# Attention pairs with two groups of keys: the gate products in two pieces of 12 instead of three of 8

## What is computed

```
y_c = chunk_band_attention(...)   # C: softmax(q k^T / 8 + bias) v, over at most 640 keys
y_a = dsa_mixer(...)              # A: softmax over the 256 best-scored of up to 1024 keys, times v
gates = sigmoid(h @ w_gate)       # 1024 x 4096, computed beside the attention
mixed = sum(gates * up, axis=branch)
```

## Time and profile before

| | before |
|---|---|
| median of 3 runs | 1749.71 us |
| the profiled execution | 1752.26 us |
| its span, first to last instruction | 1750.5 us |
| mean granted TensorE clock | 0.986 |
| TensorE matmul busy | 1683.8 us, 96% |
| VectorE busy | 1439.9 us, 82% |
| ScalarE busy | 938.0 us, 54% |
| GpSimd busy | 117.4 us, 7% |

### The profile page before, as it was taken

One profiled execution on the slowest core, in us unless ns is written; L12 is line 12 of the kernel. 1 busy time (PEld: TensorE's weight loads), 2 busy tenths in 40 slices (PEclk: granted clock), 3 DMA queues, 4 the chain that ended last, 5 costly groups with the idle time before them and its releaser, 6 DMA issues. The chain is left out here.

```text
span 1750.5 us, 24119 instructions
## 1 busy us (share of the span) xinstructions
PE 1683.8 (96%) x8776; PEld 1271.7 (73%) x8776; DVE 1439.9 (82%) x2045; ACT 938.0 (54%) x1218; POOL 117.4 (7%) x137
## 2 busy tenths in 40 slices
PE   7999999999999999999999999999999999999990
PEld 7768888877677777777778888867777777777760
DVE  6687958989799988678828986789888989898997
ACT  6533122133444545555566532277777787877762
POOL 1100000000000000000000000032211010000003
PEclk9999999999999999999999999999999999999995
DMA  5202132122354422412316841399999999999967
GB/s 210 72 1 85 54 108 92 61 85 73 108 189 131 140 69 67 145 55 67 127 37 238 304 172 66 137 381 393 403 397 404 393 404 392 404 394 402 405 270 288
DMA packets 77041, 359.82 MB, mean 206 GB/s; under 512 B 9021, under 2 KB 11613, under 8 KB 50589
## 3 DMA queue, kind: packets, MB, share of 16 engines
q1 hardware_dynamic: 67372, 325.14, 49.8%
q0 software_dynamic: 5888, 20.97, 3.5%
q10 hardware_dynamic: 3696, 12.59, 1.8%
HBM read 301.63 MB, written 55.99 MB: 204 GB/s over the span
## 5 line engine op out<-in xcount | busy, mean ns | idle before, releaser
L2805 DVE TENSOR_TENSOR wa_lo<-wa,w_hi 128x2048 fp32r<-128x2048 f32 x124 | 281.6, 2284 | 15.8 <-ACT w_hi L2689 14.9
L2689 ACT ACTIVATE w_hi<-wa 128x2048 fp32r<-128x2048 f32 x124 | 237.5, 1917 | 83.3 <-DMA wa<-expert_up 73.8
L1608 PE MATMUL psum<-h_hi,w_hi 128*128 128x512 f32 x510 | 210.0, 412 | 3.2 <-ACT gate_out L1270 2.7
L1608 PE MATMUL psum<-h_hi,w_lo 128*128 128x512 f32 x510 | 204.2, 400 | 0.0
L1608 PE MATMUL psum<-h_lo,w_hi 128*128 128x512 f32 x510 | 202.3, 397 | 0.0
L176 DVE MAX8 top<-sel 128x8 f32<-128x384 f32 (+5 forms) x192 | 171.3, 892 | 4.6
L174 DVE MATCH_REPLACE8 sel<-top,sel 128x384 f32<-128x384 f32 (+5 forms) x192 | 168.2, 876 | 0.0
L2813 DVE TENSOR_TENSOR wb_lo<-wd,w_hi 128x2048 fp32r<-128x2048 f32 x62 | 139.4, 2289 | 30.9 <-ACT w_hi L2699 30.9
L2585 PE MATMUL psum<-w_hi,xT_hi 128*96 128x512 f32 x508 | 162.2, 400 | 0.1
L2585 PE MATMUL psum<-wa_lo,xT_hi 128*96 128x512 f32 x512 | 159.8, 393 | 0.0
L2585 PE MATMUL psum<-w_hi,xT_lo 128*96 128x512 f32 x508 | 158.5, 393 | 0.0
(11 more groups left out here) (404 smaller groups left out, 3277.7 us busy)
## 6 DMA issues: line engine op xcount, KB each, us to landing
wa<-expert_up SPq DMA_DIRECT2D x128, 1024.0 KB, 24.1
wd<-expert_down SPq DMA_DIRECT2D x64, 1024.0 KB, 24.2
w<-w_gate SPq DMA_DIRECT2D x32, 512.0 KB, 4.2
gate_pre<-gate_out SPq DMA_DIRECT2D x64, 256.0 KB, 3.4
gate<-gate_pre SPq DMA_DIRECT2D x32, 512.0 KB, 5.4
ys<-yo ACTq DMA_DIRECT2D x31, 384.0 KB, 7.0
w<-w_T SPq DMA_DIRECT2D x18, 512.0 KB, 3.8
ys<-zeros SPq DMA_DIRECT2D x7, 1152.0 KB, 5.9
```

What stands on the lines that cost most here:

```text
L1608: ins = nc.tensor.matmul(psum[:, 7, :], w[:, k, :], x[:, k, half * 512:(half + 1) * 512], start=(n == 0), stop=(n == BURST - 1))
L2689: nc.scalar.activation(hi_a(i, j, q).rearrange("p c m n -> p (c m n)"), wa[j][q][:, :, :, :].rearrange("p c m n -> p (c m n)"), ACT.Copy). ...
L2805: nc.vector.tensor_tensor(wa_lo[j][q][:, :, :, :].rearrange("p c m n -> p (c m n)"), wa[j][q][:, :, :, :].rearrange("p c m n -> p (c m n)" ...
```

## The change

Pairs with one group keep three pieces of 8. In pairs with two groups the first piece has 12 gate products, the second has none and the third has 12. What stood on both sides of the second piece now follows without anything between: the turns of the first groups, the weighted sums that waited, the turns of the second groups and the weighted sums of the first groups. The number of instructions on each engine and the data are the same. In the "turned" pair too, the first piece of 12 stands ahead of the scores.

```diff
--- before.py
+++ after.py
@@ -1632,16 +1632,16 @@
             def pair(i):
 
                 u = groups[i][0]
-                part = BURST // 3
+                parts = (BURST // 3, BURST // 3) if groups[i][3] else (BURST // 2, 0)
                 turned = isinstance(groups[i - 1][0], str)
                 if turned:
-                    gate(gates_before(u), part)
+                    gate(gates_before(u), parts[0])
                 if u + 2 < NU:
                     score(u + 2, 2)
                 else:
                     weigh_waiting()
                 if not turned:
-                    gate(gates_before(u), part)
+                    gate(gates_before(u), parts[0])
                 if u == NB:
                     turn_back(NT - 1)
                 for r in range(2):
@@ -1649,7 +1649,7 @@
                     pe.wait_ge(scaled, u + r - NB + 1)
                     turn(i + r)
                 weigh_waiting()
-                gate(gates_before(u) + part, part)
+                gate(gates_before(u) + parts[0], parts[1])
                 if not groups[i][3]:
                     for r in range(2):
                         pe.wait_ge(pt_copied, i + 2 + r - 1)
@@ -1660,7 +1660,7 @@
                 waiting.append(i)
                 if u + 2 == NU:
                     weigh_waiting()
-                gate(gates_before(u) + 2 * part, part)
+                gate(gates_before(u) + sum(parts), BURST - sum(parts))
```

## The result

The changed kernel takes 1773.58 us (median of 4 runs, 1771.97 to 1775.46); the kernel before, run beside it, 1751.03 us. The ratio is 1.0114, 95% interval 1.0100 to 1.0129: slower by 1.1%. The profiled execution took 1773.39 us, its span 1771.6 us, where the forecast was 1773.7 and 1771.9. For the median the forecast was 1771.1 us in a range of 1761 to 1780; the measured one is 2.5 us above it.

The account below looks back on a forecast made before the run. TensorE was taken to bound the stretch of C and A. First pairs 14.3, second pairs 3.9 and two clock falls 3.2 us sum to +21.4 us: 1749.71 becomes 1771.1 us, range 1761 to 1780.

Parts of the forecast that it names:

- The bound: In C and A, TensorE sets the pace, so every idle microsecond the change makes is added to the time.
- The first pairs: Eight pairs, heads 0 and 1: weighted sums wait for `norm`, so the moved piece becomes idle time; 14.3 us.
- the price of a moved product: Gate products in the middle of a pair: steps of 0.232 us, so eight moved elsewhere cost 1.86 us there.
- The second pairs: Pairs with heads 2 and 3: no wait for `norm`, the limit is ScalarE's copy of the first groups; 3.9 us.
- the wait for the copy: Heads 2 and 3, C b = 5, 6, 7 and A b = 4: turns wait for ScalarE's copy; +0.3 us each.
- the turned pair: Heads 2 and 3, no waiting sums to fill the time while ScalarE copies: +0.8 us.
- the last pair: Its second group waits for copies that stand behind four `y_highs` on ScalarE: +1.9 us.
- the two covered pairs: A, b = 5 and 6, heads 2 and 3: longer sums from the pair before cover the copies; 0 and -0.1 us.
- The clock: Nine long idle times in C and A may drop the clock to 1.2 GHz: two falls taken, 3.2 us.
- Not slower: Rival: the wait for `norm` doesn't bind, only breaks go, 1.6 us, giving 1748.1 us; chance 0.07.
- A falling clock at nearly every idle time: Rival: 18.2 + 14.4 = 32.6 us, 1782.3 us; five to eight falls 1776 to 1781; chance 0.15.
- Part of the loss taken back: Rival: shorter chain or later stages absorb delay; 8 to 13 us more instead of 21, 1758 to 1763 us; chance 0.10.

Follow-up runs that it names:

- the second experiment: Pieces of 12 only in the eight pairs with heads 2 and 3, three pieces of 8 elsewhere, against the kernel before: ratio 1.0019.
- the first experiment: Pieces of 12 only in the eight pairs with heads 0 and 1 of two-group blocks, against the kernel before: ratio 1.0101.

## Why the prediction was right

**The bound.** TensorE set the pace; its new idle time, 18.4 - 2.5 = 15.9 us, and the falls came out in the span nearly one for one. No later stage took the delay back.

**The first pairs.** The step was that the wait for `norm` binds and its chain keeps its length. It keeps it to 0.01 us, and taking `exp` out of the chain takes the loss away. Forecast 14.3 us, measured 13.8 (without falls). The size is off by the price of a moved product: eight cost 1.86 us in the forecast, and 1.75 to 1.84 here.

**The second pairs.** Forecast 3.9, measured 3.6: the wait for the copy cost 0.25 us in a pair instead of 0.3, the turned pair 0.8 as forecast, the last pair 1.8 instead of 1.9, and the two covered pairs gained 0.07 each. In the last pair the wait was 1.36 us, behind the `y_highs`, as described.

**The clock.** This term was mis-sized: two falls of 1.6 us were taken, and three of 1.5 us came. The forecast couldn't say which pairs; it was chosen between one idle time with a fall and one without. The price of one was right. With 17.4 + 4.5 = 21.9 us against 18.2 + 3.2 = 21.4, the two errors nearly cancel. That the profiled execution came within 0.3 us of its forecast is luck to that extent: no row said that there would be two falls or three.

**The rivals.** Not slower: refuted, the sums waited for `norm` and not for the copy printed in the earlier trace rows; it now stands as the releaser in seven of eight first pairs. A falling clock at nearly every idle time: refuted, three of nine. By the Trainium skill, "TensorE: Matmul & The Clock Gate", section "A second HAM failure mode: psum-queue depth-cycling", short idle times between groups of matmuls can make the clock go back and forth. The three windows at 0.50 above agree that it happens, and the six idle times without a fall say that its count can't be had from the idle times. Part of the loss taken back: 0.8 us at most, outside the stretch.

**What was to be seen in the profile.** The signs came. The pairs of C with heads 0 and 1 take 12.1 us without a fall, 12.2 were named; with one they take 13.6. The waits ahead of the weighted sums were named as 1.6 to 2.1 us and are 1.57 to 2.0, the one behind the `y_highs` as 1.5 and is 1.36. The waits of 0.4 us for ScalarE's copies in the second pairs of C are there, but mostly inside the two turns, as 0.77 us instead of 0.38.

## What to carry to other kernels

Filler work between two steps covers a chain on other engines. Before it is moved, follow that chain link by link: the time from what starts it to what it releases is the least that must stand between them, and in this kernel every product taken out below that was lost in full. Where a chain is long only because of its place in another engine's list, as `norm` behind two reciprocals that it doesn't need, move it there: that one move gave 1.7 us to the kernel before and took back 19 of the change's 22.

## What the runs showed of the hardware

An idle time of TensorE of the same length can be followed by a fall of the clock or not. The 1.83 us of the earlier trace rows is one: the kernel of the second experiment has the same idle time at the same place, as TensorE's timeline shows, and the clock stays at 1.00 in the window around it.

```profile
455.80 0.47 PE L1608 MATMUL psum<-h_hi,w_hi 128*128 128x512 f32 x1 [1.83 <-ACT gate_out L1270]
```

```profile
452.00:462.00 10.00, 7.92 (x42) 5.54 (x41) 2.96 (x10) 5.13 (x11) 2.94 (x3) 1.00 0.07 26
```

Such a fall lasts 3.4 us and cost 1.5 to 1.6 us in C, where TensorE had work. It can begin with the end of the idle time, at 750.50 in the changed kernel, with the sums starting at 750.56, or later: in the first experiment the sums start at 723.63 and the clock is still 1.00 in the window 724.60 to 724.80 and 0.50 in the one from 724.90 to 728.30. Idle times of 1.2 to 1.6 us in C and A (in the changed kernel those that end at 701.7 and 861.7 us among them, 1.57 us each) weren't followed by one in any of the profiles.
